# Hybrid branch, output and gate projections as three fp32r products of parts

## What is computed

```python
h = rmsnorm(x, g_pre)
proj = h @ w_in        # q, k, v, index, conv, stick and spatial columns,
                       # gate_paths (4 x 256), merge_logits (4 x 1024)
o = stack([sparse attention, gated conv, stick-breaking attention, spatial gating])
o = o * silu(gate_paths)
z = einsum('bsnw,nwd->bsnd', o, w_branch)            # branch projection
g = sigmoid(merge_logits + b_merge)
merged = sum(g * z, axis=2)
y = merged @ w_out                                   # output projection
x = x + rmsnorm(y, g_post)
ple = p_i @ w_ple                                    # PLE projection
x = x + ple * sigmoid(x @ w_ple_gate)                # gate projection
```

## Time and profile before

| | us |
|---|---|
| median of 3 runs | 4246.2 |
| lowest, highest | 4231.04, 4247.58 |
| profiled execution, its own time | 4249.68 |
| its span in the trace | 4248.0 |
| TensorE busy | 3768.5 |
| VectorE busy | 1732.7 |
| ScalarE busy | 1224.7 |

### The profile page before, as it was taken

The page is one execution under the profiler, slowest core; times in us unless marked ns, Lnnn a source line. Parts: engine busy times, 40 slices in busy tenths (PEclk is TensorE's granted clock), DMA queues, the critical chain, the costliest instruction groups (busy, mean ns, idle before and its releaser), DMA issues.

```text
span 4248.0 us, 60025 instructions
## 1 busy us (share of the span) xinstructions
PE 3768.5 (89%) x26061; PEld 2364.1 (56%) x26061; DVE 1732.7 (41%) x3103; ACT 1224.7 (29%) x2255; POOL 462.0 (11%) x503
## 2 busy tenths in 40 slices
PE   6999979999989985488898798888989998989998
PEld 5777763433435444377786432235756755756764
DVE  3326531212242256745635312225853324854322
ACT  3226431111122266443342210003252212334211
POOL 2211020000000122210012100000102200101210
PEclk9999989999999987667898899999999999989999
DMA  7521219898863149833341599994203220212221
GB/s 250 179 77 46 83 76 365 322 368 321 321 266 117 59 147 315 246 88 99 97 128 62 216 400 420 420 420 155 80 33 122 84 104 21 80 60 85 104 89 40
DMA packets 311064, 739.21 MB, mean 174 GB/s; under 512 B 67928, under 2 KB 144224, under 8 KB 261648
## 3 DMA queue, kind: packets, MB, share of 16 engines
q1 hardware_dynamic: 299296, 697.93, 44.6%
q0 software_dynamic: 11504, 37.44, 2.6%
HBM read 673.41 MB, written 61.89 MB: 173 GB/s over the span
## 4 chain that ended last, share of the span: by engine, by line
PE 73%; DMA 10%; DVE 9%; ACT 4%; issue 1%; POOL 1%; SPq 0%; DVEq 0%; POOLq 0%; ACTq 0%
PE ps L62 70%; DMA raw<-in_moe_w_dram 7%; PE ps L66 4%; DMA b<-in_ada_w_dram 2%; DVE mx L75 1%; DVE spr L75 1%; DVE o L75 1%; DVE sT L75 1%; DMA sa<-Ad 0%; DVE b L75 0%; ACT TZ L72 0%; ACT c L72 0%; DMA c<-in_w_in_dram 0%; ACT b L72 0%; DVE cr L75 0%
## 5 line engine op out<-in xcount | busy, mean ns | idle before, releaser
L62 PE MATMUL ps<-raw,xinT 128*64 128x512 f32 (+1 forms) x4096 | 596.0, 494 | 45.1 <-DMA raw<-in_moe_w_dram 36.5
L62 PEld LDWEIGHTS ps<-raw,xinT 128*64 128x64 f32 (+1 forms) x4096 | 195.5, 124 | 426.0 <-issue 291.6
L62 PE MATMUL ps<-wp,hp 128*128 128x512 f32 x1536 | 360.8, 396 | 11.0 <-DVE wp L75 11.0
L62 PEld LDWEIGHTS ps<-wp,hp 128*128 128x128 f32 x1536 | 291.1, 190 | 78.1 <-DVE wp L75 11.4
L62 PE MATMUL ps<-raw,hidT 128*64 128x512 f32 x1024 | 241.2, 606 | 13.5 <-DMA raw<-in_moe_w_dram 13.5
L62 PE MATMUL ps<-c,hT 128*128 128x512 f32 x512 | 234.0, 608 | 3.6 <-issue 2.2
L62 PE MATMUL ps<-c,oT 128*128 128x512 f32 x512 | 222.8, 592 | 1.4 <-ACT oT L72 1.4
L62 PE MATMUL ps<-xr,b 128*128 128x512 f32 (+1 forms) x432 | 161.2, 533 | 9.2 <-ACT xr L72 4.6
L75 DVE TENSOR_TENSOR mx<-mx,ps 128x512 f32<-128x512 f32 x156 | 105.2, 685 | 156.4 <-PE ps L62 156.2
L75 DVE TENSOR_TENSOR wp<-c,wp 128x1536 fp32r<-128x1536 f32 x32 | 58.4, 1824 | 261.8 <-ACT wp L72 261.8
L62 PE MATMUL ps<-ar,naxh 128*128 128x512 f32 x576 | 147.6, 406 | 19.2 <-DVE ar L75 8.8
(11 more groups left out here) (502 smaller groups left out, 6402.5 us busy)
## 6 DMA issues: line engine op xcount, KB each, us to landing
raw<-in_moe_w_dram SPq DMA_DIRECT2D x384, 1024.0 KB, 9.3
c<-in_w_in_dram SPq DMA_DIRECT2D x28, 2048.0 KB, 7.9
mx<-in_ada_w_dram SPq DMA_DIRECT2D x14, 2048.0 KB, 7.9
b<-in_ada_w_dram SPq DMA_DIRECT2D x8, 2048.0 KB, 10.3
a<-in_na_w_qkv_dram SPq DMA_DIRECT2D x6, 2048.0 KB, 8.0
c<-in_w_branch_dram SPq DMA_DIRECT2D x16, 512.0 KB, 4.0
c<-in_w_out_dram SPq DMA_DIRECT2D x4, 2048.0 KB, 8.5
c<-in_w_ple_gate_dram SPq DMA_DIRECT2D x4, 2048.0 KB, 7.6
```

The lines of the kernel that those rows point to most:

```text
L62: return self.e.matmul(out, lhsT, rhs, start=start, stop=stop, skip_group_check=True) if self.e is not None else self
```

## The change

In both layers, the branch, output, PLE and gate projections are formed from parts. Each needs a high and a low part of its weight and of its activations: `lo` is a new tile for the low parts of oT, mT and xT, their high parts lie in `oTr`. ACT evicts the transposes as high parts, and DVE subtracts them from the PSUM bank for the low parts (before, ACT and DVE evicted half each). The merge begins with high x high products of the first half contraction for all four token groups, then low parts of h, then low parts of the weights (`first`); the transposes of o go between the groups of the second half. The output weights are loaded as `Parts` made in the merge; the first one's parts are made in its last step. `h_out` no longer waits for the merge's end before it transposes; p is transposed between the output projection's halves. The norm is a class, `HNorm`: in the first layer its high and low parts are interleaved with the evictions; in the second its first three chunks stand in the previous layer's `h_out` beside the second half of the gate products, and the fourth in `h_mix`. The result is stored in eight pieces of 128 x 512 as they are done.

Core of the diff:

```diff
 def h_merge
+        def turn(c):
             for half in range(2):
                 e.wait_ge(*P.dve.at(*k_('gated', half, c)))
                 pe_turns(...)
+        def first():
+            ...
+            for t in range(3):
+                ...                       # hhigh, high | hlow | low (DVE and POOL)
+                for i in G4:
+                    for k in range(4):
+                        ins = e.matmul(P.psum[:, b, :], (hTr if t == 1 else hp)[:, k, gs], (lo if t == 2 else hi)(0)[:, k], (t, k) == (0, 0), False)
 def place(n, q, i):
-            e.wait_ge(*ring.loaded(wb[q]))
+            e.wait_ge(*P.act.at(*k_('bhigh', q)))
+            e.wait_ge(*P.dve.at(*k_('blow', q)))
             for k in range(2):
-                ins = e.matmul(P.psum[:, b, :], oT[:, br * 2 + k, ...], ring.tile(wb[q], 2)[:, k, :], k == 0, k == 1)
+                e.matmul(P.psum[:, b, :], oTr[:, cut[0], cut[1]], high[:, k, :], k == 0, False)
+                e.matmul(P.psum[:, b, :], oTr[:, cut[0], cut[1]], low[:, k, :], False, False)
+                ins = e.matmul(P.psum[:, b, :], lo_[:, cut[0], cut[1]], high[:, k, :], False, k == 1)
+        def beside(q):                    # act; dve makes low_ and wo[0]'s low parts alike
+            e.activation(high_, raw, ACT.Copy).then_inc(*P.act.inc(*k_('bhigh', q)))
+            for m in range(4) if q == 7 else ():
+                wo[0].act(e, m)
 def h_out, pe
-        fence(P, e, k_('merge'))
+        for c in (0, 1, 2):
+            turn('mT', y, c)
+        for c in G4:
+            dense(wo[0], 'wo', 'mT', 0, c)
+            if c == 0:
+                turn('mT', y, 3)
+        for i in range(2):
+            pe_turns(P, e, k_('pT', i), ...)
+        for c in G4:
+            dense(wo[1], 'wo', 'mT', 1, c)
+        ...                               # PLE from parts, 4 groups twice
+        for c in G4:
+            turn('xT', x, c)
+        for n in range(2):
+            for c in G4:
+                dense(wg[n], 'pg', 'xT', n, c)
+                if N and n == 1 and c >= 2:
+                    N.pe_turn(e, c - 2)
 act
+        turned('mT')
+        fence(P, e, k_('merge'))
+        for m in range(4):
+            wo[1].act(e, m)
+        ...
+        for n in range(2):
+            for c in G4:
+                kept('ple', ple, n, c)
+                if n:
+                    wg[0].act(e, c)
         turned('xT')
+                for j in range(4) if m == 0 else ():
+                    wg[1].act(e, j)
+                if N and m in (4, 5):
+                    N.act_square(e, c)
+                    N.W.act(e, 2 * c)
+                    N.W.act(e, 2 * c + 1)
+                if N and m == 6:
+                    N.act_evict(e, 0)
+                    N.act_square(e, 2)
+                    N.act_high(e, 0)
 dve
+                if N and m == 4:
+                    N.dve_scale(e, 0)
+                if N and m == 5:
+                    N.W.dve(e, 0)
+                    N.W.dve(e, 1)
+                    N.dve_scale(e, 1)
+                if N and m == 6:
+                    N.W.dve(e, 2)
+                    N.dve_evict(e, 0)
+                    N.dve_scale(e, 2)
+                    N.W.dve(e, 3)
 def h_mix, act (second layer)
+            N.act_evict(e, 1)
+            N.act_square(e, 3)
+            N.act_high(e, 1)
+            N.act_evict(e, 2)
+            N.act_high(e, 2)
+            if out and n == 1:            # qkv(1)
+                N.act_evict(e, 3)
+                N.act_high(e, 3)
+                high(1)
 def h_store
-        fence(P, e, front)
-        for c in G4:
+        for n in range(2):
+            for c in G4:
+                e.dma_start(dst[c * 128:c * 128 + 128, ns], x[:, c, ns]).then_inc(*s_out.inc())
```

More of the change, by code:

```diff
@@ L233, in pe @@
             e.wait_ge(*s.at(*event))
-        for k in range(8):
-            ins = e.matmul(out, low(k), self.high[:, k], False, k == 7)
+        for k in ks:
+            ins = e.matmul(out, low(k), self.high[:, k], False, k == ks[-1])
         return ins
@@ L3196, in pe @@
         for c in G4:
[L3197 to L3204, removed]
+            N.pe_turn(e, c)
     def act(e):
@@ L3264, in dve_rope, with h_mix_order @@
     e.tensor_tensor(o2, o2, T, ADD).then_inc(*P.dve.inc(*event))
-def h_mix_order(qkv, turn, index, feat, token, conv, spatial, columns):
+def h_mix_order(late, qkv, turn, index, feat, token, conv, spatial, columns):
     for n in range(8):
@@ L3271, in h_mix_order @@
             columns()
-        if n:
+        if n == 2 and late:
+            turn(0)
+        if n > (1 if late else 0):
             turn(n - 1)
@@ L3309, in pe @@
     def pe(e):
-        fence(P, e, k_('norm'))
+        if out:
+            N.pe_turn(e, 2)
         def dense(load, g, w, key, emptied):
@@ L3383, in high @@
                 W[t].act(e, m)
-        high(1)
+        if not out:
+            high(1)
         def qkv(n):
@@ L3828, in h_merge, with in_order @@
     rows = lambda p: ring.tile(wr[p // 2])[:, 4 * (p % 2):4 * (p % 2) + 4]
-    places = [(q, i) for q in range(8) for i in G4]
-    def in_order(part, half, place):
+    branch = lambda q: (ring.tile(wb[q], 2), ring.rounded[wb[q] % ring.n][:, 2:4], ring.rounded[wb[q] % ring.n][:, 4:6])
+    def in_order(part, half, beside, place):
         part(1)
@@ L3879, in place @@
             b, free = P.banks.take(k_('branch', q, i), (P.dve,) + k_('weighed', n))
-            e.wait_ge(*ring.loaded(wb[q]))
+            raw, high, low = branch(q)
+            e.wait_ge(*P.act.at(*k_('bhigh', q)))
+            e.wait_ge(*P.dve.at(*k_('blow', q)))
             for f in free:
@@ L3915, in act @@
         part(0)
-        turn(0)
         high(1)
-        for c in (1, 2, 3):
-            turn(c)
-        in_order(part, skip, place)
+        in_order(part, half, beside, place)
         P.end(k_('merge'), P.act)
@@ new lines, in dense @@
+        def dense(part, what, turned, n, c):
+            key = k_(what, n, c)
+            b, free = P.banks.take(key, (P.act,) + key)
+            for half in range(2):
+                e.wait_ge(*P.act.at(*k_(turned, c, half)))
+            for f in free:
+                e.wait_ge(*f)
+            part.pe(e, P.psum[:, b, :], lambda k: high[:, k, toks(c)], lambda k: low[:, k, toks(c)],
+                    *[(P.dve,) + k_(turned, 'low', c, half) for half in range(2)]).then_inc(*P.pe.inc(*key))
+            if c == 3:
+                P.pe.name('weights', id(ring), part.i)
@@ new lines, in pe, with dst @@
+        P.pe.name('weights', id(ring), wp.i)
+        for c in G4:
+            turn('xT', x, c)
+        for n in range(2):
+            for c in G4:
+                dense(wg[n], 'pg', 'xT', n, c)
+                if (n, c) == (1, 3):
+                    P.end(k_('out'), P.pe)
+                if N and n == 1 and c >= 2:
+                    N.pe_turn(e, c - 2)
+    def dst(what, X, c, half):
+        return X[:, half * 4:half * 4 + 4, toks(c)], P.bank(*k_(what, c, half)).rearrange("p (j n) -> p j n", j=4)
@@ L4086, in dve @@
             e.tensor_tensor(x[:, c, :], x[:, c, :], y[:, c, :], ADD).then_inc(*P.dve.inc(*k_('xnew', c)))
+            for m in range(2) if c == 1 else ():
+                wp.dve(e, m)
+        for m in range(4):
+            wg[0].dve(e, m)
         turned('xT')
-        P.end(k_('out'), P.dve)
         for n in range(2):
```

382 lines of the change are left out of this document (249 added, 133 removed).

## The result

| | before | after |
|---|---|---|
| median (4 runs each), us | 4245.6 | 4118.7 |
| lowest, highest | 4231.0, 4247.6 | 4113.6, 4129.1 |
| ratio, 95% interval | | 0.9715, 0.9702 to 0.9728 |
| profiled execution, own time | 4249.7 | 4129.1 |
| its span | 4248.0 | 4127.4 |

The change saves 127 us of the median and 120.6 of the span. The forecast was 121.0 of the span and 4126 for the median.

What follows compares the result with a forecast made beforehand. TensorE, busy 89% of the span, was taken as the bound. Two layers' 94.6 plus 17.9, 5.6 and 2.9 gave 121.0 off the profiled 4249.7: 4128.7, or 4125 as median, rounded up to 4126; range 4110 to 4150.

Steps and rivals of the forecast that it cites:

- (a): Branch products in the merge: 32 places a layer go from 1.717 to 1.361 us, splits hidden; 11.4 us saved a layer.
- (b): Output projection: 64 fp32 products become part products, with p's transposes between its halves; net 10.5 us saved a layer.
- (c): PLE gate projection: its products go from 55.2 to 43.6 us as part products; 11.6 us saved a layer.
- (d): Merge start: first products need only high parts, so TensorE starts earlier, same 2.1 us for low clock; 5.2 saved a layer.
- (e): End of merge: the hand-over from last branch product to first output product falls from 6.1 to 3.7 us; 2.4 saved a layer.
- (f): From output to gate projection: 21.0 us falls to 14.8, with the gate weight landing after 7.6; 6.2 saved a layer.
- (g): Second layer's norm: moved beside the previous layer's gate products, 44.7 us after the last gate product falls to 26.8; 17.9 saved.
- (h): First layer's norm: high parts interleaved with evictions, so the fourth group ends at 2934 instead of 2939.6; 5.6 us saved.
- (i): Tail after the last product: results stored in half chunks as they are done, last one issued earlier; 2.9 us saved.
- The slower rival: Stationary loads of part products come into the open, 0.415 us a part: +161 us for -74, time 4361; chance 0.03.
- merge start comes back: Merge start or the oT splits stall for DVE's low parts: 10.4 us come back, time 4136; chance 0.07.
- rival of late gate weights: Gate weight fetches of 2 MB take up to 14.0 us, 6.4 over the one used, twice: time 4139; chance 0.12.

Runs made afterwards that it cites:

- four parts: The changed kernel with a fourth part product, low x low, in the output and gate projections; median 4183.2 us, ratio to before 0.9851.
- open norm: The changed kernel with the second layer's norm in the open between gate projection and first qkv product, interleaved as in the first layer; median 4138.9 us, ratio 0.9765.

## Why the prediction was right

The terms, by the same stages in both traces, in us:

| term | forecast | measured | from |
|---|---|---|---|
| (a) branch, a layer | 11.4 | 11.4 | fp32 branch: 238.0 - 226.6 |
| (b) output | 10.5 | 10.7 | 55.2 to 45.35 less 0.87 of the fourth chunk's transposes |
| (c) gate | 11.6 | 11.4 | 55.2 to 38.37 + 5.46 |
| (d) merge start | 5.2 | 6.1 | splits of h to end of branch: 244.2 to 226.7, less (a) |
| (e) end of merge | 2.4 | 2.4 | 5.9 to 2.62 + 0.87 |
| (f) output to gate | 6.2 | 6.0 | 21.0 to 3469.41 - 3454.38 = 15.0 |
| a layer | 47.3 | 48.0 | |
| (g) second norm | 17.9 | 18.1 | 44.7 to 25.7 + 0.87 |
| (h) first norm | 5.6 | 4.1 | first square to fourth qkv eviction: 43.9 to 39.8 |
| (i) tail | 2.9 | 1.9 | 11.7 to 9.8 |
| not forecast | 0 | 0.5 | first mix and attention -0.8, second 1.9, ahead of the hybrid layers -0.6 |
| sum | 121.0 | 120.6 | 2 x 48.0 + 18.1 + 4.1 + 1.9 + 0.5 |

**The sum** was met more closely than its terms: the layers gave 1.4 more than forecast, (h) and (i) 2.5 less, and stages without a forecast 0.5. That these cancel to 0.4 us is luck. What is not luck is that no term is off by more than 1.5 us and that the edits moved the stages they were meant to move.

**The price of a product**, which carries 74 of the 121, held, because it was read from two places where TensorE is the bound and its clock full. The rule weighed beside it, four passes at a part's price, would have given 94 us; four parts at 0.227, measured, show why it is too much. With that the rival in which parts save nothing is gone. The slower rival, with stationary loads in the open, would need evictions 10 us apart; they are 5.44.

**What hides** was right: the branch splits cost nothing even three times over.

**(d)** was under by 0.9. The price taken for the low clock was 2.1 us and is 1.4; the rest is rounding of products (864 of them took 195.86 us, 0.3 less than at 0.227). It has a second lesson, that the rival "merge start comes back" was priced from the kernel before, 5.2 a layer, while the old order with parts costs 9.9.

**(f)** was right in its size and in its cause, and it is the thinnest place of the change. The weight landed in 7.64 us against 7.6 taken, and 15.0 us between the projections against 14.8. The rival of late gate weights was priced at its lateness, up to 6.4 us a layer; the doubled fetch shows 7.9 us for 5.1. Landings of 9.0 to 9.3 us in the first layer of three related runs cost 1.4 to 2.9. So this rival did not occur in the changed kernel's trace and occurs, in a small size, in single executions of its relatives.

**(g)** was right within 0.2. The queue of DVE kept its order, and the open norm's 14 us show what it is worth.

**(h)** is mis-sized, since its working was incomplete. It had the late rotations, with transposes at 2921.9 (measured 2922.5, in a trace whose first square is 0.6 later), and left out that TensorE's wait for them brings a low clock for the next group: 7.08 us for 5.45. That is the 1.5 us missing. (d) had priced the low clock after its idle time, (h) did not.

**(i)** is mis-sized too, in what stands behind the stores. The last one leaves POOL at 4119.90, 2.3 us after the last product, as forecast; landings of the eight:

```profile
DMA to landing us min/median/max: 2.3/2.3/3.4
```

That is even less than the 3.1 that the sum used. But from 4119.90 + 2.3 = 4122.2 to the span's end at 4127.4 are 5.2 us in which the trace has no transfer and no work of an engine. In the kernel before, the last store left at 4239.15 and landed at the latest 5.4 later, 3.5 us before the end. The forecast held this rest to be the same in both; it grew by 1.7. It belongs to the change and not to one execution, for from the last gate eviction to the end it is 9.8 us in the traces of all nine kernels that store in eight pieces. Why, the traces don't show.

**The median** was 7 us below the forecast although the span's difference was met within half a us. The forecast took over from the kernel before that a profiled execution lies 3.5 us over the median; in the changed kernel it was 10.4. Only one execution of each kernel is traced, so this can't be followed up for the others. Across the ten kernels the spread lies ahead of the hybrid layers: the first square stood at 2895.8 in the one profile, 2896.4 in the other, and down to 2879.1 in others, while the hybrid stages repeat.

## What to carry to other kernels

Read the price of each form of product where TensorE is the only bound and multiply; it held to 2% here, where counting passes gave a quarter too much. Then walk each hand-over through the queues of the other engines, and give a wait of TensorE of about 2 us two prices, its length and nearly twice its length, since the group behind it ran at a lower clock in some traces and not in others. Compare the edited stages and not only medians, when an untouched part of the kernel moves more between executions than the edits do.

## What the runs showed of the hardware that was not expected

- A short wait of TensorE can have a price beyond its length, and its length doesn't tell. After 1.89 us the clock was 0.77 and the group took 7.08 us instead of 5.45; after 2.03 us (branch as fp32) 0.68 and 7.32. But after 2.10 us (four parts) and 2.24 us (open norm), at the very place of the 2.03, and after 1.97 in front of the PLE products of the kernel before, it was 1.00, as after 0.7. What decides is open.
- A part product costs its columns and some 13 ns. For 512 columns 227 ns are measured; for 256 columns the token evictions of the kernel before stand 2.88 us apart for 24 products:

```profile
3047.63 0.39 ACT L72 ACTIVATE tok<-ps 128x256 f32<-128x256 f32 x1 [2.50 <-PE ps L62]
3050.51 0.38 ACT L72 ACTIVATE tok<-ps 128x256 f32<-128x256 f32 x1 [2.49 <-PE ps L62]
3053.39 0.38 ACT L72 ACTIVATE tok<-ps 128x256 f32<-128x256 f32 x1 [2.50 <-PE ps L62]
```

  That is 120 ns. The 256 columns between the two cost 107 ns, 0.42 each, one cycle at 2.4 GHz; so 512 columns are 213 ns, and some 13 ns remain at either size. The load of 128 columns, 188 ns, is longer than such a product and still doesn't set the distance. An fp32 product, 859 ns, is four times 213 and 6 more. So what splitting pays is 13 ns a part, and what it saves is 213 ns a product. Where the 13 ns come from is open.
- The landing time of the same 2 MB weight, with the same neighbours in the program, was 7.6 to 7.9 us in five traces and 9.0 to 9.3 in three, and with one more transfer ahead of it 12.7.
